# A decoder trunk step in float32 pieces on one core: the down projection of the later token blocks as seven block products

## The reference

```python
def conv_ffn(h, prev, w_a, w_b, conv_w, conv_b, w_down):
    a = h @ w_a                                   # 1024 -> 2816
    b = h @ w_b
    ext = jnp.concatenate([prev.astype(a.dtype), a], axis=1)
    ac = conv_b + sum(conv_w[j] * ext[:, j:j + T] for j in range(CONV_W))
    y = (jax.nn.gelu(ac, approximate=False) * b) @ w_down     # 2816 -> 1024
    return y, ext[:, -(CONV_W - 1):].astype(prev.dtype)
```

## Time and profile before

| | us |
|---|---|
| median of 3 runs | 2571.65 (2567.12 to 2578.09) |
| span of the profiled execution, first to last instruction | 2573.1 |
| TensorE busy in it | 2489.9 (97%) |
| VectorE, ScalarE, GpSimd busy | 1207.3, 717.0, 449.7 |
| mean granted clock of TensorE | 0.987 |
| DMA, mean over the span | 190 GB/s |

### The profile page before, as it was taken

The page is one execution under the profiler, slowest core; times in us unless marked ns, Lnnn a source line. Parts: engine busy times, 40 slices in busy tenths (PEclk is TensorE's granted clock), DMA queues, the critical chain, the costliest instruction groups (busy, mean ns, idle before and its releaser), DMA issues.

```text
span 2573.1 us, 36513 instructions
## 1 busy us (share of the span) xinstructions
PE 2489.9 (97%) x13263; PEld 2109.4 (82%) x13263; DVE 1207.3 (47%) x2297; ACT 717.0 (28%) x1457; POOL 449.7 (17%) x331
## 2 busy tenths in 40 slices
PE   7898999999999999999999999999999999999997
PEld 7778789999777888888887888888887887888886
DVE  6968465333346864221246774221236774321234
ACT  4214232222223332111233342211233342211133
POOL 4526246555550110000000020000000020000000
PEclk9979999999999999999999999999999999999999
DMA  7641357776757424555656423555655623455653
GB/s 250 215 149 51 125 199 267 249 261 249 278 211 268 156 87 165 191 192 183 237 196 227 183 83 131 213 191 185 235 196 196 231 99 131 180 191 184 234 201 134
DMA packets 145350, 489.03 MB, mean 190 GB/s; under 512 B 8881, under 2 KB 79778, under 8 KB 96025
## 3 DMA queue, kind: packets, MB, share of 16 engines
q1 hardware_dynamic: 136747, 482.58, 52.0%
q10 hardware_dynamic: 8472, 4.75, 0.6%
HBM read 375.45 MB, written 112.02 MB: 189 GB/s over the span
## 4 chain that ended last, share of the span: by engine, by line
PE 88%; DVE 6%; issue 2%; DMA 2%; ACT 1%; POOL 1%; SPq 0%; DVEq 0%; ACTq 0%
PE ps L567 23%; PE ps L569 23%; PE ps L568 22%; PE ps L633 11%; PE ps L788 3%; PE ps L614 1%; PE ps L813 1%; DMA w_both<-w_split 1%; PE ps L820 1%; POOL w_both L543 0%; DVE arena L2022 0%; PE ps L926 0%; PE ps L598 0%; DVE arena L1838 0%; DVE arena L2054 0%
## 5 line engine op out<-in xcount | busy, mean ns | idle before, releaser
L567 PE MATMUL ps<-h_hi,w_both 128*128 128x512 f32 (+1 forms) x1536 | 586.8, 382 | 3.1 <-issue 3.1
L569 PE MATMUL ps<-h_lo,w_both 128*128 128x512 f32 (+1 forms) x1536 | 583.2, 380 | 0.0
L568 PE MATMUL ps<-h_hi,w_both 128*128 128x512 f32 (+1 forms) x1536 | 579.5, 377 | 0.0
L568 PEld LDWEIGHTS ps<-h_hi,w_both 128*128 128x128 f32 x1536 | 288.8, 188 | 58.9
L569 PEld LDWEIGHTS ps<-h_lo,w_both 128*128 128x128 f32 x1536 | 288.3, 188 | 59.5
L567 PEld LDWEIGHTS ps<-h_hi,w_both 128*128 128x128 f32 x1536 | 288.2, 188 | 59.0 <-issue 4.0
L567 PE MATMUL ps<-w_both,act_hi 128*128 128x512 f32 (+1 forms) x748 | 297.4, 398 | 2.0 <-DVE x_tok L2136 1.8
L569 PE MATMUL ps<-w_both,act_hi 128*128 128x512 f32 (+1 forms) x748 | 296.2, 396 | 0.0
L568 PE MATMUL ps<-w_both,act_lo 128*128 128x512 f32 (+1 forms) x748 | 295.4, 395 | 0.0
L2213 DVE TENSOR_TENSOR act_lo<-arena,act_hi 128x512 fp32r<-128x512 f32 (+1 forms) x176 | 139.2, 793 | 328.3 <-ACT act_hi L1527 327.9
L633 PE MATMUL ps<-h_hi,w_both 128*128 128x304 f32 (+1 forms) x1664 | 288.7, 296 | 2.0 <-ACT arena L1333 0.8
(11 more groups left out here) (252 smaller groups left out, 3284.2 us busy)
## 6 DMA issues: line engine op xcount, KB each, us to landing
w_both<-w_split SPq DMA_DIRECT2D x288, 1024.0 KB, 4.8
w_split<-w_both SPq DMA_DIRECT2D x96, 1024.0 KB, 6.2
w_raw<-in_w_down SPq DMA_DIRECT2D x24, 512.0 KB, 4.3
w_raw<-in_w_a SPq DMA_DIRECT2D x22, 512.0 KB, 4.2
w_raw<-in_w_b SPq DMA_DIRECT2D x22, 512.0 KB, 4.2
w_raw<-in_w_in SPq DMA_DIRECT2D x20, 512.0 KB, 4.5
x_tok<-in_x_prompt SPq DMA_DIRECT2D x16, 512.0 KB, 7.0
arena<-in_x_prompt SPq DMA_DIRECT2D x16, 512.0 KB, 6.9
```

The lines of the kernel that those rows point to most:

```text
L567: nc.tensor.matmul(out, lhs[0], rhs[0], start=first, stop=False)
L568: nc.tensor.matmul(out, lhs[1], rhs[0], start=False, stop=False)
L569: return nc.tensor.matmul(out, lhs[0], rhs[1], start=False, stop=last)
```

## The change

In blocks 1 to 3 the down projection becomes seven block products (the scheme of Strassen and Winograd, one level). Tokens, features and output columns are halved: a11, a12, a21, a22 are quarters of the activations (11 feature tiles by 256 tokens), b11 to b22 quarters of the weights. Sums of quarters stand in for eight products. Product 1 is a11 by b11, 2 is a12 by b21, 3 is s4 by b22, 4 is a22 by a sum of weights, 5 to 7 are s1, s2, s3 by sums of weights. A product has 11 steps, a step 6 matmuls; there are 77 steps in 42 groups (chunks of two steps, the last of one).

- The four sums of weights are made once, in block 0, in 22 pieces between its 24 units: loaded by SyncE (`sums_in`), summed by VectorE (`t_sums`), rounded by ScalarE (`sums_high`), subtracted by GpSimd (`sums_low`), stored by SyncE (`sums_out`), through two buffers. The final gain is loaded behind the last store. The down projection's own units are no longer stored.
- In later blocks eight half slots replace the four, and SyncE loads finished sums (512 KB) or raw quarters (256 KB, for products 1 to 3), which GpSimd splits each time (`k_parts`).
- VectorE makes s1 to s4 (`sums`) and the low pieces (`part_low`), ScalarE the high pieces (`part_high`). ScalarE copies product 1 out of PSUM (`first_copied`), and VectorE adds the copy where it is wanted (`first_adds`). Products 2 and 7 go on in the banks of 1 and 6.
- `Fori` loops around this code become written-out loops, and some semaphores are merged.

```diff
+PRODUCT_ORDER = ([(p, c) for c in range(len(CHUNKS)) for p in (1, 5)]
+         + [(p, c) for c in range(len(CHUNKS)) for p in (6, 2)]
+         + [(p, c) for c in range(len(CHUNKS)) for p in ((3, 7, 4) if c == len(CHUNKS) - 1 else (3, 4, 7))])
+K_STEPS = [(g, p, CHUNKS[c][0] + j, j) for g, (p, c) in enumerate(PRODUCT_ORDER) for j in range(CHUNKS[c][1])]
+PRODUCT_BANK = {1: 4, 2: 4, 5: 6, 4: 6, 6: 0, 7: 0, 3: 2}
+GOES_ON = (2, 7)
+PLAIN_WEIGHTS = {1: (0, 0), 2: (1, 0), 3: (1, 1)}
+T_PLACE = {5: 0, 7: 1, 4: 2, 6: 3}
+STEPS = len(K_STEPS)
+PLAIN_STEPS = [q for q, (g, p, k, j) in enumerate(K_STEPS) if p in PLAIN_WEIGHTS]
...
+def k_slot(q):
+    return k_place(q) % 8
...
+SUMS_BEHIND = {-1: [("s1", 0)]}
+for _c in range(1, len(CHUNKS)):
+    SUMS_BEHIND.setdefault(2 * _c - 1, []).append(("s1", _c))
+for _c in range(len(CHUNKS)):
+    SUMS_BEHIND.setdefault(9 + 2 * _c, []).extend([("s3", _c), ("s2", _c)])
+for _c in range(len(CHUNKS)):
+    SUMS_BEHIND.setdefault(21 + 3 * _c, []).append(("s4", _c))
...
+def left(k, n, half):
+    return acts[:, k:k + n, HEAD + 256 * half:HEAD + 256 * (half + 1)]
...
+def left_operand(p, c):
+    k, n = CHUNKS[c]
+    return {1: lambda: left(k, n, 0), 2: lambda: left(HALF_K + k, n, 0), 3: lambda: left(HALF_K + k, n, 0),
+            4: lambda: left(HALF_K + k, n, 1), 5: lambda: s1(c), 6: lambda: left(k, n, 0),
+            7: lambda: left(k, n, 1)}[p]()
...
-        if not isinstance(u, int) or u >= 3:
+        if not isinstance(u, int) or 3 <= u < U_DOWN + 2:
...
+    def first_down():
+        quarters = w_down.rearrange("(a k p) (c n) -> k p a c n", a=2, p=P, c=2)
+        def sums_in(g):
+            if g >= 2:
+                sp.wait_ge(t_stored[g % 2], 4 * U_DOWN + 32 * (g // 2))
+            at = slice(256 * (g % 2), 256 * (g % 2 + 1))
+            for a in range(2):
+                sp.dma_start(t_buf[g % 2][:, 0, 512 * a:512 * (a + 1)].rearrange("p (c n) -> p c n", c=2),
+                             quarters[g // 2, :, a, :, at]).then_inc(t_loaded[g % 2], 16)
+        def sums_out(g):
+            sp.wait_ge(t_lo_ready, g + 1)
+            at = slice(256 * (g % 2), 256 * (g % 2 + 1))
+            for l in range(2):
+                sp.dma_start(t_split[:, :, g // 2, l, at].rearrange("t p n -> p t n"),
+                             t_buf[g % 2][:, l, :].rearrange("p (t n) -> p t n", t=4)).then_inc(t_stored[g % 2], 16)
+        for m in range(24):
+            n, i = m // 12, m % 12
+            k = 2 * i if i < 10 else 20
+            unit(0, m % 4, U_DOWN + m, (U_DOWN + m) // 4, raw(m % 4, 2), wdown[:, k:k + 2, n * 512:(n + 1) * 512]
+                 if i < 8 else wdown[:, (16, 18, 20, 20)[i - 8]:(16, 18, 20, 20)[i - 8] + 2, n * 512:(n + 1) * 512])
+            if m >= 3:
+                sums_out(m - 3)
+            if 1 <= m <= 2 * HALF_K:
+                sums_in(m - 1)
+            if m == 7:
+                sp.wait_ge(conv_out_taken, 18)
+                for t in range(TILES):
+                    x_rows(0, t)
+        sums_out(2 * HALF_K - 1)
+        for x in range(2):
+            sp.wait_ge(t_stored[x], 4 * U_DOWN + 32 * HALF_K)
+        final_gain()
+    def later_down(b):
+        for q, (g, p, k, j) in enumerate(K_STEPS):
+            slot = k_slot(q)
+            if k_before(q) is None:
+                sp.wait_ge(unit_done, b * UNITS + U_DOWN - 3 + slot // 2)
+            else:
+                sp.wait_ge(k_done, b * (STEPS - 1) + (k_before(q) + 2 - STEPS))
+            if p in PLAIN_WEIGHTS:
+                a, c = PLAIN_WEIGHTS[p]
+                sp.dma_start(k_given[:, slot, :],
+                             w_down[(HALF_K * a + k) * P:(HALF_K * a + k + 1) * P, 512 * c:512 * (c + 1)]).then_inc(
+                                 k_loaded[slot], 16)
+            else:
+                if q < 4:
+                    for x in range(2):
+                        sp.wait_ge(t_stored[x], 4 * U_DOWN + 32 * HALF_K)
+                sp.dma_start(k_slots[:, slot].rearrange("p a n -> p (a n)").bitcast(F32),
+                             t_split[T_PLACE[p], :, k, :, :].rearrange("p a n -> p (a n)")).then_inc(k_loaded[slot], 16)
+            if q == NEXT_X_AT[0]:
+                sp.wait_ge(act_ready, FT * (b + 1))
+            if q in NEXT_X_AT:
+                x_rows(b, NEXT_X_AT.index(q))
+            if q == 50:
+                final_gain()
...
-    for j in range(U_OUT // 4, UNITS // 4):
+    for j in range(U_OUT // 4, U_DOWN // 4):
         units(j)
-    with pool.Fori(1, BLOCKS) as b:
+    def sums_low(g):
+        pool.wait_ge(t_hi_ready, g + 1)
+        t = t_buf[g % 2]
+        nc.gpsimd.tensor_tensor(t[:, 0, :].bitcast(F32R), t[:, 0, :], t[:, 1, :], ALU.subtract).then_inc(t_lo_ready, 1)
+    for m in range(24):
+        if m >= 3:
+            sums_low(m - 3)
+        units(U_DOWN // 4 + m // 4, (m % 4,))
+    sums_low(2 * HALF_K - 1)
+    def k_parts(b):
+        for r, q in enumerate(PLAIN_STEPS):
+            slot, n = k_slot(q), len(PLAIN_STEPS)
+            given, hi, lo = k_given[:, slot, :], k_slots[:, slot, 1, :], k_slots[:, slot, 0, :]
+            pool.wait_ge(k_loaded[slot], k_load(b, q))
+            nc.gpsimd.tensor_scalar(hi, given, 1.0, 1.0, ALU.mult, ALU.mult).then_inc(w_hi_ready, 1)
+            pool.wait_ge(w_hi_ready, n * b + (UNITS + r + 1 - n))
+            nc.gpsimd.tensor_tensor(lo, given, hi.bitcast(F32), ALU.subtract).then_inc(w_ready, 1)
+    for b in range(1, BLOCKS):
         ahead(b)
+        k_parts(b)
...
+    def down_by_halves(b):
+        for q, (g, p, k, j) in enumerate(K_STEPS):
+            slot, bank0 = k_slot(q), PRODUCT_BANK[p]
+            if j == 0:
+                pe.wait_ge(act_lo_ready, GROUPS * b + (2 * FT + g + 1 - GROUPS))
+            if k == 0:
+                if p == 6:
+                    pe.wait_ge(act_ready, FT * (b + 1))
+                if p == 2:
+                    pe.wait_ge(first_copied, b)
+                if p == 4:
+                    pe.wait_ge(part_added, 10 * b - 6)
+                if p == 7:
+                    pe.wait_ge(part_added, 10 * b - 4)
+            if p in PLAIN_WEIGHTS:
+                pe.wait_ge(w_ready, len(PLAIN_STEPS) * b + (UNITS + PLAIN_STEPS.index(q) + 1 - len(PLAIN_STEPS)))
+            else:
+                pe.wait_ge(k_loaded[slot], k_load(b, q))
+            for t in range(2):
+                cols = slice(256 * j + P * t, 256 * j + P * (t + 1))
+                last = three(ps[:, bank0 + t, :], (act_hi[:, g % 2, cols], act_lo[:, g % 2, cols]),
+                             (k_slots[:, slot, 1, :], k_slots[:, slot, 0, :]), k == 0 and p not in GOES_ON,
+                             k == HALF_K - 1, goes_on=p in GOES_ON)
+                if t == 0 and q in (71, 73, 75):
+                    last.then_inc(unit_done, 21 if q == 71 else 1)
+            if q == STEPS - 1:
+                last.then_inc(unit_done, 1)
+            else:
+                last.then_inc(k_done, 1)
+            if q == step_end(g) and g - ROWS_AT in (0, 3, 6, 9):
+                t = (g - ROWS_AT) // 3
+                if t == 0:
+                    pe.wait_ge(x2_ready, 8 * b + 4)
+                row_transposes(8 * b + 8, t, 4, 1)
...
+        def sums_high(g):
+            act.wait_ge(t_ready, g + 1)
+            t = t_buf[g % 2]
+            nc.scalar.copy(t[:, 1, :].bitcast(F32R), t[:, 0, :]).then_inc(t_hi_ready, 1)
+        def first_pairs():
+            for n in range(2):
+                for i in range(FT // 2):
+                    if (n, i) > (0, 0):
+                        pair(n, i, i == 0)
+                        sums_high(11 * n + i - 1)
...
+        def part_high(g):
+            p, c = PRODUCT_ORDER[g]
+            if p in SUM_OF:
+                act.wait_ge(sum_ready, SUMS * b + (SUM_ORDER.index((SUM_OF[p], c)) + 1 - SUMS))
+            elif p == 2 and c == 0:
+                act.wait_ge(act_ready, FT * (b + 1))
+            elif p == 1 and c == 0:
+                act.wait_ge(act_ready, FT * b + 20)
+            if g >= 2:
+                act.wait_ge(k_done, b * (STEPS - 1) + (step_end(g - 2) + 2 - STEPS))
+            nc.scalar.copy(part_of(act_hi, g), left_operand(p, c)).then_inc(act_hi_ready, 1)
...
+        def later_parts():
+            for g in range(2, GROUPS):
+                part_high(g)
+                if g == 12:
+                    act.wait_ge(k_done, b * (STEPS - 1) + (product_end(1) + 2 - STEPS))
+                    nc.scalar.copy(first_part, ps[:, 4:6, :]).then_inc(first_copied, 1)
+                if g in SQUARES_BEHIND:
+                    next_square(SQUARES_BEHIND[g])
+                if g == 20:
+                    nc.scalar.preload_act_table_set("natural_log_exp_and_others")
+                    next_guess()
+                t, half = (g - ROWS_AT - 2) // 3, (g - ROWS_AT - 2) % 3
+                if 0 <= t < TILES and half < 2:
+                    next_rows_high(t, half)
...
+    def sums(b, g):
+        for kind, c in SUMS_BEHIND.get(g, ()):
```

(62 more changed lines are left out.)

267 lines of the change are left out of this document (179 added, 88 removed).

## The result

The changed kernel takes **2655.8 us** (2652.7 to 2659.0), the kernel before 2569.4 beside it: a ratio of 1.0326, 95% interval 1.0304 to 1.0349. Slower, as forecast, by nearly twice as much as forecast: the spans differ by 81.2 us (2654.3 against 2573.1), where the sum said 45.2. The measured median lies in the range, 0.2 us inside the upper end of the forecast's own.

What follows compares the result with a forecast made beforehand. TensorE, busy for 97% of the span, was taken as the bound. 24.2 + 29.5 + 10.5 - 18.0 - 1 = +45.2 on 2573.1 gave 2618.3, median 2617 us; range 2568 to 2668, the forecast's own 2591 to 2656.

Steps and rivals of the forecast that it cites:

- Matmuls of the later blocks: Later down projections: 66 of 528 matmuls go, 15.4 us a block gained if operands are there in time.
- Operands of the later blocks: Later down projections: VectorE and GpSimd shut each other out, so 9.4 of 15.4 us a block are lost.
- First half of block 0: Block 0's down projection, first half: turns of the loop through a buffer delay units, +24.2 us (10.8 to 31.2).
- the term for the rows of x: Block 0's down projection, first half: loading rows of x between the four turns adds 3 us.
- turns of 15.4 and 19.0: Block 0's loop through a buffer: one turn takes 15.4 us, or 19.0 with a unit's split ahead of the sums.
- Second half: Block 0's down projection, second half: units take 10.0 us each (9.0 to 11.0), +29.5 us (18.5 to 40.5).
- a rival of 0.05: Block 0's down projection: the clock falls to the 1.2 GHz level in the gaps, +19 us, so 2636; chance 0.05.
- Boundary: Between block 0 and block 1: the next unit queues behind last store and final gain, +10.5 us (8 to 13).
- What costs nothing: Whole kernel: written-out loops and merged semaphores count for nothing, as no wait of TensorE hangs on them.
- Sums hidden: Block 0: making the sums delays no unit, only 8 us at the boundary remain, so 2536 us; chance 0.10.
- Lower bounds everywhere: Whole kernel: every loss at its lower bound, 37.3 - 43.1 - 1, so 2565 us, no change; chance 0.13.
- Later blocks lose as well: Later blocks: late low pieces cost more than the 66 matmuls, +5 us a block, so 2650; chance 0.12.

Runs made afterwards that it cites:

- e3b: Changed kernel, but later blocks load finished weights in place of the raw quarters, so GpSimd splits nothing there: 2626.8 us, ratio 1.0213.
- e1: Changed kernel with the four loads of the next rows of x issued earlier in block 0, ahead of the store of piece 2: 2651.1 us, ratio 1.0318.
- e14: Changed kernel with three piece buffers, pieces stored one unit later (two in the second half), rows of x fetched one per unit: 2637.6 us, ratio 1.0251.
- e13: Changed kernel with down projections' splits on ScalarE and VectorE instead of GpSimd, three piece buffers, later stores, several loads and operations reordered: 2548.9 us, ratio 0.9922.
- e2: Changed kernel without the sums of weights in block 0; later blocks load finished units of other weights of the same size: 2572.5 us, ratio 1.0015.

## Why the prediction was right, and where it was not

The sign and the mechanisms were right; the sum was 36.0 us too small. That the median still lies in the forecast's own range, by 0.2 us, is luck: the four runs differ by 6.3. By the steps of the sum:

- **Matmuls of the later blocks** (15.4 us each): e3b shows it, 111.7 where 110.9 was worked out.
- **Operands of the later blocks** (9.4 lost): right in size and cause. Against e3b the three blocks lose 8.4, 11.7 and 8.7; 12 matmuls 0.43 us apart in block 2 and 6 in block 3, at the low clock, are 2.3 and 1.2 us of that. The split among the groups was off: 7.8 of block 1's gaps are in products 6 and 2 (5.7 given), hardly any in 3, 4 and 7 (3.7 given). That an operation with two SBUF inputs waits for GpSimd's whole instruction, read from the earlier trace rows alone, carried this part, and the 33 operations of block 1 show it.
- **First half of block 0** (+24.2, bound 31.2): +39.9, the step that failed, by the term for the rows of x. SyncE's loads of pieces 2, 4, 6, 8 and 10 stand right behind the stores of pieces 0, 2, 4, 6 and 8, so they show the turns:

```profile
641.59 1.21 SPq L599 DMA_DIRECT2D arena<-in_w_down  x2
...
663.08 1.21 SPq L599 DMA_DIRECT2D arena<-in_w_down  x2
...
681.51 1.21 SPq L599 DMA_DIRECT2D arena<-in_w_down  x2
...
714.47 1.21 SPq L599 DMA_DIRECT2D arena<-in_w_down  x2
...
732.45 1.21 SPq L599 DMA_DIRECT2D arena<-in_w_down  x2
```

  The first store is done 18.4 us behind the first matmul, where 19.6 was worked out. The four turns take 21.5, 18.4, 33.0 and 18.0, where 18.0 each was taken: three are 3.9 too long in all, and the one with the rows of x in it 15.0, for which 3 was put. It is not a term one can add by itself, though: e1 took half of that pause away and got 6.3 of this half back. In e14, with three buffers, a later queue and the rows one per unit, this half takes 104.6. Two readings were off as well: the earlier trace rows has the low piece done 2.2 us behind the unit, not 1.7, and turns of 15.4 and 19.0 put into the sum give 13.8 to 28.2, not 10.8 to 31.2. The formula of the Trainium skill, "DMA: Bandwidth & Descriptors", Anatomy of one DMA, that stands outside the sum is given there for transfers on GpSimd's path; these are SyncE's, and the shortest turn measured, 18.0, does not bear it out.
- **Second half** (+29.5, bound 40.5): +35.8, inside its bounds. "I take 10.0" a unit; (119.8 - 3.5) / 11 is 10.6, with units 9.8 to 11.3 apart. I had added one ring at a time and put TensorE's 6.98 into it at the full clock. The experiments speak for several rings of like length that share VectorE, GpSimd and SyncE's queue, and the clock fell as well: 57 matmuls of this half start 0.43 us apart, not 0.23, against 8 before, and 49 x 0.194 is 9.5 us, more than the 6.3 that are missing; 24 in the first half are 4.7 more. In the stretch from 733.70, behind a pause of 3.79 us, the granted clock is 0.50, the level of 1.2 GHz, with TensorE busy throughout. I had this as a rival of 0.05 with a price of 19. It should have been in the sum: once units are late every few microseconds, pauses such as that of the earlier trace rows are part of the forecast, not another case.
- **Boundary** (+10.5): +9.4, by the way described (queue, store, final gain, 1 MB). e13 takes it to 2.3.
- **What costs nothing**: the prediction said that no wait of TensorE hangs on the loops. 11.4 us lie outside the down projections: 3.9 at the turn of the loop (below), and 7.5 in other stages, of which 26 matmuls behind the longer pauses, 0.43 apart, make 5.0 (26 x 0.194). The rest, some 0.8 a block, I have not traced.
- **Rivals.** Sums hidden: no, though e13 shows that the stage holds them. Lower bounds everywhere: no. Later blocks lose as well: not in their down projections, but with the 11.4 us outside them all they gain is 3.5 us, and e2 puts it at nothing (1.0015).

## What to carry to other kernels

Before work goes to GpSimd because it is idle, look at what VectorE does meanwhile: if it has two inputs in SBUF, the two engines hold each other up (25 us of one stage here), and the same work on VectorE can cost less than half (689 against 1464 ns). When work is put into a stage that has one long chain per unit, list every ring (buffers, each in-order queue, each pair of engines that exclude one another) with its length and its period; here one shortened gave 7 to 10 us, and two together 35.5. An issue that waits should stand behind the loads that TensorE needs, not ahead of them. Fewer matmuls pay only as far as everything that feeds them keeps up.

## What the runs showed of the hardware that I had not expected

**A jump back to the head of the loop takes 3.6 to 6.5 us on TensorE's sequencer**, over all runs, and hides only behind matmuls already queued: in every run the next matmul starts 0.3 to 0.4 us behind its end. The branch of blocks 1 to 2, before and then after (line, sequencer, operation: duration ns min/median/max, first and last start):

```profile
L1170 PEldq COMPARE_BRANCH  x1: 4851/4851/4851, 1371.2 to 1371.2; - x1
```

```profile
L1384 PEldq COMPARE_BRANCH  x1: 4935/4935/4935, 1454.1 to 1454.1; - x1
```

Before, it was reached 3.5 us ahead of the last matmul's end (1374.7), after, 1.7 us ahead (1455.8), since the last steps now wait for their pieces; that makes the pause 3.38 us in place of 1.48. In e13 the branch is reached 1.6 us ahead and takes 6.4, and the pause is 5.0. What makes its length differ was not tried. The Trainium skill, "Runtime: NRT & Kernel Launch", Instruction fetch mechanics, has a taken branch out of the loaded pages wait for a fetch of its target; no run here shows that fetch, only the length of the branch.

**Stores take up to twice as long beside other transfers**: 1 MB of a unit landed in 4.7 us alone, the 1 MB of a piece in 5.81 us in the chain of the changed kernel. In e1 it took 9.31 us where the 2 MB of rows are under way, and 7.55 us beside the next piece's and the next raw unit's loads, 1 MB issued just ahead of it.
